# Where the weighted values of prompt attention stand in TensorE's order

## What is computed

```
def block(args):
    i, q_b, g_b, fq_b, c_b = args
    ...
    o_n = nsa_block(q_b, qpos, g_b, kc, vc, cpos, ks, vs, ov, kw_b[:, :, 0], kw_b[:, :, 1], wpos, tb)
    o_f = fox_block(fq_b, qpos, c_b, fk, fv, c, kpos)
    return o_n, o_f
...
l = jnp.einsum('bthd,bshd->bhts', q, k) * scale        # scores
p = masked_softmax(l + bias, mask)                     # probabilities
o = jnp.einsum('bhts,bshd->bthd', p, v)                # weighted values
```

## Time and profile before

| | |
|---|---|
| median of three runs | 2355.24 us (2354.65 to 2360.14) |
| the profiled execution | 2357.64 us |
| its span, from first to last instruction | 2355.8 us |
| PE busy (matmuls) | 2297.8 us, 98% |
| DVE busy | 1211.1 us, 51% |
| ACT busy | 545.9 us, 23% |
| POOL busy | 832.4 us, 35% |
| mean granted clock of TensorE | 0.997 |

### The profile page before, as it was taken

One profiled execution on the slowest core, in us unless ns is written; L12 is line 12 of the kernel. 1 busy time (PEld: TensorE's weight loads), 2 busy tenths in 40 slices (PEclk: granted clock), 3 DMA queues, 4 the chain that ended last, 5 costly groups with the idle time before them and its releaser, 6 DMA issues.

```text
span 2355.8 us, 33102 instructions
## 1 busy us (share of the span) xinstructions
PE 2297.8 (98%) x12215; PEld 1508.8 (64%) x12215; DVE 1211.1 (51%) x3023; ACT 545.9 (23%) x1300; POOL 832.4 (35%) x874
## 2 busy tenths in 40 slices
PE   8999999999989999999999999999999999999999
PEld 4444566666666666788884478888888874443343
DVE  4886627787854444224226873334433334239765
ACT  0000116787743331111112121111111100001131
POOL 0000005565651003666633634333333436203541
PEclk9999999999999999999999999999999999999999
DMA  5422821031078886222316111111111126434101
GB/s 186 114 76 73 294 87 63 2 113 33 2 207 248 242 251 224 81 81 81 90 63 174 44 37 55 37 37 54 37 36 39 53 90 210 157 129 153 55 18 58
DMA packets 185963, 240.41 MB, mean 102 GB/s; under 512 B 53436, under 2 KB 128834, under 8 KB 184266
## 3 DMA queue, kind: packets, MB, share of 16 engines
q1 hardware_dynamic: 181018, 218.99, 30.1%
q0 software_dynamic: 3616, 9.73, 1.3%
q10 hardware_dynamic: 1168, 9.58, 1.2%
HBM read 216.18 MB, written 37.99 MB: 108 GB/s over the span
## 4 chain that ended last, share of the span: by engine, by line
PE 57%; DVE 2%; ACT 1%; issue 0%; DVEq 0%; ACTq 0%
PE ps L2255 37%; PE ps L2419 11%; PE ps L2308 5%; PE ps L2476 2%; PE ps L2406 1%; DVE xT L152 1%; PE ps L2484 1%; ACT xT L2529 0%; PE ps L2312 0%; DVE arena L3007 0%; ACT arena L2626 0%; DVE stats L2681 0%; PE ps L2351 0%; DVE queries L3010 0%; DVE arena L1400 0%
## 5 line engine op out<-in xcount | busy, mean ns | idle before, releaser
L2255 PE MATMUL ps<-xT,arena 128*128 128x272 f32 x1920 | 472.7, 393 | 1.3 <-DVE arena L1411 1.3
L2255 PEld LDWEIGHTS ps<-xT,arena 128*128 128x128 f32 x1920 | 363.9, 190 | 77.0 <-DVE arena L1411 1.7
L2255 PE MATMUL ps<-queries,arena 128*128 128x272 f32 x1312 | 332.5, 393 | 1.8 <-DVE queries L2822 1.0
L2255 PEld LDWEIGHTS ps<-queries,arena 128*128 128x128 f32 x1312 | 249.6, 190 | 53.9 <-DVE queries L2822 1.4
L235 PE MATMUL ps<-arena,xT 128*128 128x512 f32 (+1 forms) x512 | 198.2, 550 | 1.6 <-issue 0.8
L235 PEld LDWEIGHTS ps<-arena,xT 128*128 128x128 f32 x512 | 97.9, 192 | 101.5 <-issue 93.4
L2255 PE MATMUL ps<-arena 128*128 128x272 f32 x576 | 148.5, 394 | 0.5 <-DVE arena L1402 0.5
L979 ACT ACTIVATE arena<-arena 128x640 f32<-128x640 f32 (+10 forms) x208 | 136.8, 659 | 33.9 <-DVE arena L929 26.2
L2419 PE MATMUL ps<-arena 128*128 128x512 f32 x312 | 140.6, 599 | 0.0
L816 PE MATMUL ps<-arena,queries 64*128 64x512 f32 (+9 forms) x704 | 132.8, 442 | 3.6 <-DVE arena L929 2.6
L2419 PE MATMUL ps<-xT,arena 128*128 128x512 f32 x304 | 131.4, 592 | 0.0
(11 more groups left out here) (361 smaller groups left out, 3381.2 us busy)
## 6 DMA issues: line engine op xcount, KB each, us to landing
arena<-in_cache_fox_kv SPq DMA_DIRECT2D x72, 256.0 KB, 4.3
arena<-in_w_ffn_down SPq DMA_DIRECT2D x68, 256.0 KB, 3.4
arena<-in_w_in SPq DMA_DIRECT2D x16, 1024.0 KB, 5.3
xT<-in_w_ffn_down SPq DMA_DIRECT2D x64, 256.0 KB, 3.7
xT<-in_cache_fox_kv SPq DMA_DIRECT2D x56, 256.0 KB, 6.9
arena<-in_cache_nsa_kv SPq DMA_DIRECT2D x64, 192.0 KB, 8.3
arena<-in_w_ffn_up SPq DMA_DIRECT2D x11, 1024.0 KB, 5.4
arena<-in_w_ffn_gate SPq DMA_DIRECT2D x11, 1024.0 KB
```

The source lines that it names most:

```text
L2255: mm = pe.matmul(ps[:, first + BANK_OF[z], 0:PIECE], weight[:, j, :], moving[:, j, :], start=(j == 0 and z in (1, 6, 5, 7)), stop=(j == kk ...
```

## The change

Both parts of a pair's weighted values are now formed at the end of round n + 1 of TensorE's order, for the pair of round n. The call behind the last round that is then empty is left out. Nothing else is edited: the instructions, the other engines' orders and all semaphores are the same.

```
             def values_beside(n):
-                for part in (1, 0):
-                    q = n - 1 - part
-                    if 0 <= q < NPAIR and PAIRS[q].j == 1:
-                        weighted_values(PAIRS[q], part)
+                if 0 <= n - 1 < NPAIR and PAIRS[n - 1].j == 1:
+                    for part in range(2):
+                        weighted_values(PAIRS[n - 1], part)
...
                 values_beside(p.n)
             values_beside(NPAIR)
-            values_beside(NPAIR + 1)
```

## The result

The changed kernel takes 2382.77 us (median of 4 runs, 2381.49 to 2387.47) beside 2357.69 for the kernel before (4 runs, 2354.65 to 2360.56): 25.1 us more, a ratio of 1.0111 [1.0099, 1.0123] (in brackets the 95% interval, here and below). Forecast were 2373 us, +17.6. Its profiled execution was its longest, 2387.47 us, with a span of 2385.6.

The account below looks back on a forecast made before the run. Prompt attention was taken as bound by four engines waiting on each other in a ring. Terms 7.0 + 5.5 + 7.1 + 0 - 0.35 - 1.65 gave +17.6 us, so 2373 us; range 2358 to 2390, the likeliest case's own 2363 to 2385.

Parts of the forecast that it names:

- Kind A: Odd rounds of tiles 6, 5, 7: next transposes wait for ACT's copy queued behind an exponential; 7.0 us lost.
- Kind B: Odd rounds 41 to 49, 89 to 93: later scores delay DVE's logits and the next scores; 5.5 us lost.
- Kind C: Rounds like 55, 67, 79: scores, logits, inverse, POOL's scaling take 3.47 us in sequence, delaying the round after next; 7.1 lost.
- The rest ... comes out near zero: Nine other odd rounds a turn: few products, even round behind waits for POOL or DVE anyway; 0, at most 7 either way.
- The model round 86: Example for the remaining odd rounds: its second half waits 0.47 us for POOL, so moving PE's products changes nothing.
- The tail: Last products at the stage's end: start earlier, -0.35 us, and no longer run at half clock, -1.65.
- Rival 1: Other engines finish their queues in the long even round, so nothing shows; some +4 us, 2359; chance 0.17.
- rival 2: Faster by 45 fewer ends of product runs on PE, 0.16 us each: -7.2, with the tail 2346 us; chance 0.06.
- Rival 3: Clock falls behind emptied odd rounds of kind A, 1.65 us each in 12 rounds: +20, 2393 us; chance 0.11.
- a ring of engines: Prompt attention: PE, DVE, ACT, POOL each wait a little for each other; weighted values fill PE's waits, 79.3 + 39.9 us.

Follow-up runs that it names:

- the copy-first run: Changed kernel with ACT's second copy placed ahead of the exponential in odd rounds: 2393.27 us, ratio 1.0143.
- the FOX run: Kernel before, with only the FOX pairs' values formed in one run and SLC and WIN left in two parts: 2371.88 us, ratio 1.0069.
- "the rest" merged: Kernel before, with both parts in one run only for the 18 runs that the prediction took as free: 2361.81 us, ratio 1.0021.
- the last experiment: Kernel before, with both value parts cut in two around the second transposes where the scores two rounds on are at most 300 columns wide: 2353.05 us, ratio 0.9987.
- three versions that moved pieces into waits: Kernel before, part 1 in odd rounds wholly ahead of second transposes (2363.26 us) or halved around them (2355.92); both parts cut where next scores are narrow (2353.05).
- both parts in the odd round: Changed kernel with the one run of both parts a round later, in the odd round, none in the even one: 2377.44 us, ratio 1.0081.
- SLC and WIN merged: Kernel before, with only the SLC and WIN pairs' values formed in one run and FOX left in two parts: 2377.08 us, ratio 1.0083.
- half of the products: Changed kernel without the second half of each pair's key tiles in the weighted values: 2352.32 us, ratio 0.9983.
- earlier copies: Changed kernel with ACT's copies of finished values one round earlier (VALUES_BEHIND 1 for 2): 2387.23 us, ratio 1.0125.
- kind A alone: Kernel before, with both parts in one run only for 12 runs whose odd round's transposes wait for ACT's second copy: 2366.32 us, ratio 1.0044.

## Why the forecast was right in direction and too low

*Kind A* held: odd rounds of 2.72 us after 2.78 forecast, the copy behind the exponential as the limit (the copy-first run), 7.9 us instead of 7.0. The excess is some 0.4 a turn, most of it in round 6, which waits a little more behind an emptied round 5 (2.66 for 2.35).

*Kind B* was 7.6 us instead of 5.5. The mechanism was right; what was taken off for DVE catching up in the long rounds was not: 1.1 for the 1.7 us of products of rounds 41 and 43, and again of 89 and 91, 0.8 for the 1.28 of 47, 0.6 for the 0.86 of 93. The loss reached the upper bound that the text gave, the moved products themselves, some 7.5. Where nothing was taken off it came out: round 49 was to lose 1.07 and lost 1.09 in the FOX run.

*Kind C*: 7.1 forecast, 7.35 left over in the sum, 8.5 in the FOX run. The chain of 3.47 us held, and rounds 7 and 19 lost what was forecast (1.4 and 1.3); round 31 and its like lost 1.5 where 0.85 was forecast, and why is open.

*"The rest ... comes out near zero"* is the step that failed: 4.7 us, 18 rounds with 0.26 each, inside the stated bound of 7 but not at the middle. The model round 86 was read for the wait of its transposes on POOL, and that wait did stay; the scores of round 83 (and 35, whose rounds have the same lengths) hang on logits as in kind B, and that was not looked at. It has over half of the miss of 27.55 - 19.6 = 7.95 us (4.7 the rest, 2.1 B, 0.9 A, and 0.3 C as the remainder).

*The tail* was to give 2.0 us back, 1.65 of it by the clock. In the profiled execution it did not. The last products stood at the lower level, 1.2 GHz, as before, and now so did the 24 ahead of them, which took 2.96 us in round 52:

```profile
695.49 4.64 PE L862 MATMUL ps<-xT,arena 128*64 128x256 f32 x24
...
702.57 4.07 PE L853 MATMUL ps<-xT,arena 128*64 128x128 f32 x40 [0.69 <-ACT queries L992]
```

The reason given, 24 products ahead of them in one run, was no reason: that run fell too. Whether it falls is not fixed by the code of the tail: with FOX, kind A or "the rest" merged the last rounds, 94 and 95, do the same as before's, and the profiled execution shows no fall in them, so the 1.65 belonged to the one execution of before that was read, and others need not have it. The other 0.35 was not there either: where no clock fell, rounds 94 and 95 take 9.57 us with before's tail (the FOX run) and 9.50 with the changed one (the copy-first run). So the stage's +29.2 is 27.55 at round 94 and +1.65 behind it; the medians differ by 25.1, since the profiled execution was the longest of four (the others lie at 2381.5 to 2384.0).

*Rival 1* (nothing shows) and *rival 2* (fewer ends of runs gain 7.2) fell; the last experiment has more ends and is faster. The Trainium skill ("TensorEngine Tiling (Array Packing)", Key Properties) names a drain of TensorE at each change of tiling mode; the 0.16 us at the end of a run agrees, and no run here shows that fewer of them shorten this stage. *Rival 3* (clock falls in mid-stage) has no place in the changed kernel's profile, but a real one in its neighbours', as the last section shows. The prediction counts two odd rounds that had no products; there are three (1, 9 and 57), and with the tail's round 95 the emptied rounds are 45 all the same.

## What to carry to other kernels

In a ring of engines, work that nobody waits for is worth most where its engine would wait: in two parts, those of before's products that were left out had cost about a quarter of their time, in one run nearly all of it. Not every wait pays: of three versions that moved pieces into waits one gained. Before such work is moved, each round that it leaves must be read for every chain that leaves that round (copies, banks freed by the reader of the scores, scalings), not only for the wait that shows today. And where rounds repeat to 0.02 us, the starts of rounds in two traces tell apart causes that medians with a spread of 5 us can't, once each fall of the clock in either trace is allowed for.

## What was not expected of the hardware

The granted clock fell to 0.50 in mid-stage in all six experiments that emptied the rounds of the tiles of kind A (6, 5 and 7), each time right behind an emptied round (at 375.9 us with both parts in the odd round, where the even ones are empty; 386.2 with SLC and WIN merged, 378.5 and 538.9 with half of the products, 385.9 and 560.0 with earlier copies, 554.2 and 595.2 with the copy first, 540.1 with kind A alone). It fell in none of the six in which these rounds kept their products. What PE did ahead of it was transposes, scores and waits of 0.3 to 0.9 us, as at the end of round 3 with half of the products, behind which 12 products took 2.83 us instead of 1.51:

```profile
379.18 2.83 PE L862 MATMUL ps<-xT,arena 128*64 128x256 f32 x12
```

The changed kernel empties the same rounds, and its profile shows no fall before its last two rounds. Each kernel was profiled in one execution, so it is a risk and no certainty. The Trainium skill ("TensorE: Matmul & The Clock Gate", Part 4) says that a transpose doesn't count as busy time of PE in the same way as other work; the runs agree with it and as well with gaps as the cause, since no run separates the two. A run's mean clock and its time go together: of before's 22 runs those at 0.999 took 2354.4 to 2355.7 us, those at 0.995 2359.0 and 2362.8.
